# x's half of each state-space group and B and C projected as columns: the weights as stationary operand, 256 tokens moving

## The chip, the cores and the metric

One core of a Trainium2 chip runs the whole layer. The metric is the device time of one execution in microseconds (us). Five engines work beside each other and meet at semaphores: TensorE (PE in the profile, its weight loads PEld), VectorE (DVE), ScalarE (ACT), GpSimd (POOL) and SyncE (SP, which issues DMAs).

## What is computed

A decoder layer over 256 tokens of width 2048, in float32: a combined input projection, a Mamba-2 state-space branch beside a differential attention branch, gates, an output projection and a SwiGLU. The change concerns the input projection of the state-space branch and the convolution behind it:

```python
h = rms_norm(x, mix_norm_w[layer], NORM_EPS)
proj = jnp.einsum('bsd,dn->bsn', h, w_in[layer])
z, xbc, dt_raw, q, k, v, g_ssm, g_att = jnp.split(proj, splits, axis=-1)
...
xbc = jax.nn.silu(causal_depthwise_conv(xbc, conv_w, conv_b))
xs, Bm, Cm = jnp.split(xbc, [SSM_D_INNER, SSM_D_INNER + G * N], axis=-1)
```

The convolution has four taps along the tokens and is separate for each of the 6144 channels of xbc: 4096 of x (8 groups of 512), 1024 of B and 1024 of C.

## The kernel before, in words

**Products in three parts.** Every float32 matrix is split into a high part, rounded to float32r, and a low part, the rest. A product is three matmuls: high by high, high by low, low by high. The normed tokens h are kept transposed, as `h_hi` and `h_lo` (128 channels on the partitions, 16 k-tiles, 256 tokens); the norm's factor of each token (`x_rstd`, a column over tokens) is applied to the product afterwards, since h is stored without it.

**Units.** The weights stream in units of two k-tiles by 512 columns (`UK` = 2, `CW` = 512, 512 KB). SyncE loads a unit to `w_raw`, ScalarE rounds it to `w_hi` (`split_hi`, line 722), VectorE subtracts to get `w_lo` (`split_lo`, line 1246), TensorE multiplies (`rows_unit`, line 2233). Each of these has a ring of four slots (`RING` = 4): a split waits until the unit four before it is through TensorE, a load until its slot is split. A chunk is 8 units (`UPC`): 512 output columns for all 256 tokens, in one of two accumulators `acc[0]`, `acc[1]` in PSUM (two banks each, one for each 128 tokens). `acc_free` guards them. ScalarE and VectorE run through the units four ahead of TensorE (`LEAD` = 4); in their programs the end of a chunk (`chunk_done`) stands behind the split of the fourth unit of the next one.

In `rows_unit` the tokens are stationary: for each k-tile and each 128 tokens, three matmuls with 128x128 stationary tokens and 512 moving weight columns, 12 matmuls a unit. The result has tokens on the partitions ("rows").

**The order of the program.** q and k (8 chunks), v (in a form with seven products), then 8 chunks with the 16 attention heads' work between their units: first four chunks of B and C, then four of gates. Then four chunks of a projection of the attention's result, then the groups: for each of 8 groups a chunk of x in `acc[0]` and a chunk of z in `acc[1]`, the repeated ones in a loop of 7. Then the second gates, the projections and the SwiGLU. Between the units of a chunk small pieces of other work are put in by hand (`heads_between`, `branch_between`, `z_between`, `tail_between`).

**From rows to channels.** The convolution needs the channels on the partitions. So for B and C ScalarE copies `acc` to `bc_row`, scaled by `x_rstd`; some chunks later TensorE transposes it in pieces of 128x128 into the PSUM tile `side` (`bc_columns`, after the third unit of each of the four chunks of the attention's projection), ScalarE computes the first tap out of `side` (`conv_first_taps`, line 836) and VectorE the other three (`conv_other_taps`, line 1436). For x ScalarE copies `acc[0]` to `x_proj` (line 956), TensorE transposes `x_proj` back into `acc[0]` after the first unit of the z chunk (`z_between`, u == 0, eight transposes), and the taps read `acc[0]`, which is released after the last tap. A transpose is line 2249 in the profile.

**What follows in a group** (`z_between`, `z_chunk`, `x_chunk`). Still at u == 0 TensorE computes C by B (`cb`, lines 2572 and 2573) and transposes `y_row`, the normed result of the group before, which waits for VectorE's `tail_normed` (line 1611), that for GpSimd's rsqrt, and that for ScalarE's squares. VectorE's taps come behind its split of the fifth z unit. Behind them come ScalarE's silu and exponentials (`exps`, line 968), VectorE's `decays` (line 1645) and `xdt` (line 1669), ScalarE's copy to `y_row` and GpSimd's step on it (line 2186), each between splits. In the next x chunk, behind the third and fourth unit, TensorE runs the y products (`y_products`, line 2534) and VectorE `tail_gated`. GpSimd masks the decays of the next group (line 2180) meanwhile.

**dt** has 64 channels and is projected before the change as columns already (line 2463): 64 stationary weight columns, 256 moving tokens.

## Time and profile before

| | us |
|---|---|
| median of 3 runs (lowest, highest) | 2055.84 (2054.61, 2057.56) |
| the profiled execution, its own time | 2056.46 |
| its span in the trace | 2054.8 |
| TensorE busy | 2046.9 |
| TensorE's weight loads busy | 1688.1 |
| VectorE busy | 1565.0 |
| ScalarE busy | 1164.2 |
| GpSimd busy | 170.3 |

The span is divided among stages: q and k, v, attention with B, C and the first gates to about 500 us, the attention's projection to about 594 us, the groups from 594 to 1029 us, and from there the second gates, projections and the SwiGLU. Busy times of TensorE are from modelled ends: what one matmul costs is read from the distance of two starts. A group of instructions gives a line of the kernel, an engine, an operation and tiles, as `out<-in`, its count and the mean of one. A timeline row gives start, length and what was waited for; neighbouring rows of one kind are merged (x8).

### The profile page before, as it was taken

The numbers are of one execution on the slowest core, as the hardware profiler recorded it, in microseconds if no ns is written. First come the engines' busy times: TensorE is split into PE (matmuls) and PEld (weight loads), VectorE is DVE, ScalarE is ACT, GpSimd is POOL, SyncE is SP. The second block draws the span as 40 slices with busy tenths as digits, with TensorE's granted clock in tenths as the row PEclk, the third lists the DMA queues.
The fourth block names the chain that finished last, engine by engine and source line by source line (L and its number), as shares of the span: only waits on it lengthen the run. The fifth ranks groups of instructions, "written<-read, shape, count | busy, mean of one in ns | idle before, by whom it ended". The sixth has DMA issues, their size and how long they took to land.

```text
span 2054.8 us, 27952 instructions
## 1 busy us (share of the span) xinstructions
PE 2046.9 (100%) x9530; PEld 1688.1 (82%) x9530; DVE 1565.0 (76%) x1860; ACT 1164.2 (57%) x1488; POOL 170.3 (8%) x195
## 2 busy tenths in 40 slices
PE   9999999999999999999999999999999999999999
PEld 8888877778888888888888888888888888887887
DVE  6777866665866777777767887898898889877866
ACT  5444655555556666666655454566666666645543
POOL 1121000000011222222100000000000000000000
PEclk9999999999999999999999999999999999999999
DMA  7656675554566665555565657598888888666574
GB/s 250 198 180 205 194 215 165 173 168 144 183 204 184 184 184 184 184 184 184 165 193 184 211 169 246 174 306 246 258 253 239 251 257 250 198 202 229 180 240 153
DMA packets 220627, 419.80 MB, mean 204 GB/s; under 512 B 16450, under 2 KB 22003, under 8 KB 220291
## 3 DMA queue, kind: packets, MB, share of 16 engines
q1 hardware_dynamic: 212162, 399.48, 61.1%
q0 software_dynamic: 7776, 18.94, 4.3%
q8 instruction: 47, 0.77, 0.2%
q10 hardware_dynamic: 608, 0.34, 0.1%
q14 instruction: 34, 0.27, 0.0%
HBM read 410.25 MB, written 4.26 MB: 202 GB/s over the span
## 4 chain that ended last, share of the span: by engine, by line
PE 97%; DVE 2%; DMA 1%; ACT 0%; issue 0%; SPq 0%; DVEq 0%; ACTq 0%
PE acc L2233 75%; PE side L2320 9%; PE acc L2320 6%; PE side L2249 3%; PE side L2534 1%; DVE w_lo L2025 1%; PE side L2389 1%; DMA w_raw<-in_w_ffn_down 1%; DVE w_raw L1940 0%; DMA x_row<-in_x 0%; PE side L2540 0%; PE acc L2249 0%; PE side L2463 0%; ACT w_hi L1205 0%; PE side L2404 0%
## 5 line engine op out<-in xcount | busy, mean ns | idle before, releaser
L1246 DVE TENSOR_TENSOR w_lo<-w_raw,w_hi 128x1024 fp32r<-128x1024 f32 x332 | 418.9, 1277 | 250.1 <-ACT w_hi L722 248.9
L722 ACT ACTIVATE w_hi<-w_raw 128x1024 fp32r<-128x1024 f32 x332 | 347.9, 1057 | 373.1 <-PE acc L2233 319.4
L2233 PE MATMUL acc<-w_hi,h_hi 128*128 128x512 f32 x1248 | 498.4, 399 | 0.2
L2233 PE MATMUL acc<-w_hi,h_lo 128*128 128x512 f32 x1248 | 487.2, 390 | 0.0
L2233 PE MATMUL acc<-w_lo,h_hi 128*128 128x512 f32 x1248 | 486.0, 389 | 0.0
L2233 PEld LDWEIGHTS acc<-w_hi,h_hi 128*128 128x128 f32 x1248 | 234.4, 188 | 51.0 <-issue 5.6
L2233 PEld LDWEIGHTS acc<-w_hi,h_lo 128*128 128x128 f32 x1248 | 234.2, 188 | 50.4
L2233 PEld LDWEIGHTS acc<-w_lo,h_hi 128*128 128x128 f32 x1248 | 234.7, 188 | 47.9 <-issue 1.9
L1919 DVE TENSOR_TENSOR w_lo<-w_raw,w_hi 128x1024 fp32r<-128x1024 f32 x136 | 165.3, 1222 | 38.0 <-ACT w_hi L1126 35.4
L1042 ACT ACTIVATE w_hi<-w_raw 128x1024 fp32r<-128x1024 f32 x110 | 116.4, 1060 | 116.1 <-PE acc L2233 71.5
L1126 ACT ACTIVATE w_hi<-w_raw 128x1024 fp32r<-128x1024 f32 x136 | 142.9, 1057 | 66.4 <-PE acc L2233 50.9
L1205 ACT ACTIVATE w_hi<-w_raw 128x1024 fp32r<-128x1024 f32 x102 | 107.6, 1060 | 106.6 <-DMA w_raw<-in_w_ffn_down 56.4
L1721 DVE TENSOR_TENSOR w_lo<-w_raw,w_hi 128x1024 fp32r<-128x1024 f32 x110 | 132.5, 1223 | 45.6 <-ACT w_hi L1042 43.6
L1126 ACT ACTIVATE w_hi<-side_raw 128x1024 fp32r<-128x1024 f32 x100 | 106.2, 1062 | 96.6 <-PE acc L2233 45.8
L2025 DVE TENSOR_TENSOR w_lo<-w_raw,w_hi 128x1024 fp32r<-128x1024 f32 x102 | 122.6, 1223 | 48.7 <-ACT w_hi L1205 47.5
L2233 PE MATMUL acc<-w_hi,x2T_hi 128*128 128x512 f32 x384 | 150.7, 392 | 0.0
L2233 PE MATMUL acc<-w_hi,x2T_lo 128*128 128x512 f32 x384 | 149.6, 390 | 0.0
L2233 PE MATMUL acc<-w_lo,x2T_hi 128*128 128x512 f32 x384 | 149.4, 389 | 0.0
L1919 DVE TENSOR_TENSOR w_lo<-side_raw,w_hi 128x1024 fp32r<-128x1024 f32 x100 | 122.2, 1222 | 17.9 <-ACT w_hi L1126 16.3
L2233 PE MATMUL acc<-w_hi,a_hi 128*128 128x512 f32 x252 | 98.2, 390 | 0.0
L2233 PE MATMUL acc<-w_hi,a_lo 128*128 128x512 f32 x252 | 98.1, 389 | 0.0
L2233 PE MATMUL acc<-w_lo,a_hi 128*128 128x512 f32 x252 | 98.0, 389 | 0.0
(434 smaller groups left out, 3458.6 us busy)
## 6 DMA issues: line engine op xcount, KB each, us to landing
w_raw<-in_w_in SPq DMA_DIRECT2D x320, 512.0 KB, 4.3
w_raw<-in_w_ffn_down SPq DMA_DIRECT2D x88, 512.0 KB, 4.9
w_raw<-in_w_ffn_gate SPq DMA_DIRECT2D x68, 512.0 KB, 4.5
w_raw<-in_w_ffn_up SPq DMA_DIRECT2D x68, 512.0 KB, 5.3
w_raw<-in_w_ssm_proj SPq DMA_DIRECT2D x64, 512.0 KB, 4.4
side_raw<-in_w_ffn_up SPq DMA_DIRECT2D x40, 512.0 KB, 4.6
w_raw<-in_w_attn_proj SPq DMA_DIRECT2D x32, 512.0 KB, 3.7
w_raw<-in_w_out SPq DMA_DIRECT2D x32, 512.0 KB, 4.8
```

The source lines that it names most:

```text
L722: nc.scalar.activation(w_hi[:, r], w_raw[:, n % RING], ACT.Copy).then_inc(hi_ready, 1)
L1042: nc.scalar.activation(w_hi[:, unit.slot % RING], w_raw[:, source], ACT.Copy).then_inc(hi_ready, 1)
L1126: nc.scalar.activation(w_hi[:, unit.slot % RING], ffn_source(names, name), ACT.Copy).then_inc(hi_ready, 1)
L1205: nc.scalar.activation(w_hi[:, unit.slot % RING], w_raw[:, source], ACT.Copy).then_inc(hi_ready, 1)
L1246: nc.vector.tensor_tensor(w_lo[:, r], w_raw[:, n % RING], w_hi[:, r].bitcast(F32), ALU.subtract).then_inc(lo_ready, 1)
L1721: nc.vector.tensor_tensor(w_lo[:, r], w_raw[:, source], w_hi[:, r].bitcast(F32), ALU.subtract).then_inc(lo_ready, 1)
L1919: nc.vector.tensor_tensor(w_lo[:, r], ffn_source(names, names[n]), w_hi[:, r].bitcast(F32), ALU.subtract).then_inc(lo_ready, 1)
L2025: nc.vector.tensor_tensor(w_lo[:, r], w_raw[:, source], w_hi[:, r].bitcast(F32), ALU.subtract).then_inc(lo_ready, 1)
L2233: done = nc.tensor.matmul(acc[p][:, t], a[:, k0 + kk, cut], w[:, r, kk], start=first and kk == n == 0, stop=last and kk == UK - 1 and n == ...
L2249: return nc.tensor.transpose(out_at, in_, ident)
L2320: done = nc.tensor.matmul(out_at, a, w[:, r, kk], start=first and kk == n == 0, stop=last and kk == UK - 1 and n == 2, skip_group_check=se ...
L2389: last = nc.tensor.matmul(side[:, 1 + m, first:first + width], qkT[half, 0, q * P:(q + 1) * P], qkT[half, 1, 0:width], start=True, stop=True)
```

## The change

B, C and x are projected as columns from the start. `columns_unit` takes 128 weight columns as the stationary operand and all 256 tokens as the moving one: for each of 2 k-tiles, 4 column tiles and 3 products one matmul of 128x256, 24 a unit. The result has channels on the partitions, two column tiles in each bank of `acc`. VectorE multiplies it by the token factors, which now have to stand as a row on all partitions (`rstd_row`, `x_rstd_row`), and writes `bc_cols` or `x_cols` in SBUF; the taps read these. The transposes, ScalarE's scaled copies and the waits for them go. `acc[0]` is released after VectorE's product, not after the last tap. The row of factors is made once: VectorE puts `x_rstd` on diagonals, TensorE multiplies them by ones (`rstd_rows`, after the seventh unit of the second chunk), ScalarE copies the result out of `side`.

```diff
+                    if second and u == UPC - 1:
+                        act.wait_ge(rows_T, 2)
+                        act.wait_ge(norms_in, 3 * 16)
+                        nc.scalar.activation(rstd_row[:], side[:, 1, 0:T], ACT.Copy).then_inc(cols_ready, 1)
...
                 for c in range(2):
                     chunk_with_heads(i * 4 + 2 * c)
-                    for t in range(TT):
-                        last = nc.scalar.activation(bc_row[:, t, bass.ds(i * (2 * CW) + c * CW, CW)], acc[c][:, t], ACT.Copy,
-                                                    scale=x_rstd[:, t:t + 1])
-                    last.then_inc(acc_free[c], 1)
...
+            nc.scalar.activation(x_rstd_row[:], rstd_row[:], ACT.Copy).then_inc(acs_ready, 1)
...
-                chunk_done()
-                for t in range(TT):
-                    last = nc.scalar.activation(x_proj[:, t], acc[0][:, t], ACT.Copy, scale=x_rstd[:, t:t + 1])
-                last.then_inc(x_rows_ready, 1)
...
-                        act.wait_ge(x_T, g + 1)
+                        act.wait_ge(x_cols_ready, g + 1)
                         for n in range(CT):
-                            last = conv_first_taps(sums(0)[:, n], g * CT, conv_x[:, n], n)
+                            last = conv_first_taps(x_cols[:, n], g * CT, conv_x[:, n], n)
...
+                    if second and u == LEAD + 1:
+
+                        dve.wait_ge(rstd_ready, TT)
+                        for t in range(TT):
+                            last = nc.vector.tensor_scalar(rstd_diag[:, t], ident, x_rstd[:, t:t + 1], None, ALU.mult)
+                        last.then_inc(lam_sums, 1)
...
                 for c in range(2):
                     chunk_with_heads(i * 4 + 2 * c)
+                    chunk_done()
+                    nc.vector.tensor_tensor(bc_cols[:, bass.ds(i * (2 * CT) + c * CT, CT)], sums(c),
+                                            rstd_row[:].unsqueeze(1).broadcast_to([P, CT, T]), ALU.mult).then_inc(bc_cols_ready, 1)
+                    dve.wait_ge(bc_cols_ready, i * 2 + (c + 1))
+                    nc.vector.sem_inc(acc_free[c], 1)
...
+                dve.wait_ge(mm_done, unit.now(-LEAD))
+                nc.vector.tensor_tensor(x_cols[:], sums(0), x_rstd_row[:].unsqueeze(1).broadcast_to([P, CT, T]), ALU.mult).then_inc(x_cols_ready, 1)
+                dve.wait_ge(x_cols_ready, g + 1)
+                nc.vector.sem_inc(acc_free[0], 1)
...
-                    if u == 2:
-
-                        dve.wait_ge(conv_done, g + 1)
-                        nc.vector.sem_inc(acc_free[0], 1)
...
+            def columns_unit(p, k0, first, last):
+
+                r = unit.slot % RING
+                pe.wait_ge(lo_ready, unit.step())
+                for kk in range(UK):
+                    for n in range(CT):
+                        cut = slice(n * P, (n + 1) * P)
+                        for m, (w, a) in enumerate(((w_hi, h_hi), (w_hi, h_lo), (w_lo, h_hi))):
+                            done = nc.tensor.matmul(acc[p][:, n // 2, n % 2 * T:(n % 2 + 1) * T], w[:, r, kk, cut], a[:, k0 + kk],
+                                                    start=first and kk == m == n % 2 == 0, stop=last and kk == UK - 1 and m == 2,
+                                                    skip_group_check=True)
+                done.then_inc(mm_done, 1)
...
+            def rstd_rows():
+                pe.wait_ge(lam_sums, 3)
+                for t in range(TT):
+                    last = nc.tensor.matmul(side[:, 1, t * P:(t + 1) * P], ones[:], rstd_diag[:, t], start=True, stop=True)
+                last.then_inc(rows_T, 1)
...
-                        chunk(c, h_hi, h_lo, between=heads_between(i * 4 + (8 * n + 2 * c)))
+                        if n == 0:
+                            chunk_of_columns(c, between=heads_between(i * 4 + (8 * n + 2 * c)))
+                        else:
+                            chunk(c, h_hi, h_lo, between=heads_between(i * 4 + (8 * n + 2 * c)))
...
-                    if u == 2:
-                        bc_columns(c)
...
-                        pe.wait_ge(x_rows_ready, g + 1)
-                        for n in range(CT):
-                            for t in range(TT):
-                                at_col = (n % 2) * T + t * P
-                                last = transpose(acc[0][:, n // 2, at_col:at_col + P], x_proj[:, t, n * P:(n + 1) * P])
-                        last.then_inc(x_T, 1)
                         pe.wait_ge(bT_ready, g + 1)
...
-            chunk(0, h_hi, h_lo)
+            chunk_of_columns(0)
             chunk(1, h_hi, h_lo, between=z_between(0, True))
             with repeat(pe, G - 1, [(unit, 2 * UPC), (pair, 1)]) as i:
-                chunk(0, h_hi, h_lo, between=tail_between(i))
+                chunk_of_columns(0, between=tail_between(i))
                 chunk(1, h_hi, h_lo, between=z_between(i + 1))
```

In the order of instructions TensorE has in the repeated group, around the end of the first z unit, before the change (line 2233 is the row form's matmul, stationary operand last; 2249 a transpose; ISA and REGISTER_ALU compute addresses and counts):

```order
L2233 MATMUL acc<-w_hi,h_lo 128x512
L2558 REGISTER_ALU
L2249 MATMUL acc<-ident,x_proj 128x128 x8
L2572 ISA
L2572 MATMUL side<-bc,bT 128x256
L2573 ISA
L2573 MATMUL side<-bc,bT 128x128
L2249 MATMUL side<-ident,y_row 128x128 x8
```

and the same place of the changed program:

```order
L2249 MATMUL acc<-w_hi,h_lo 128x512
L2597 REGISTER_ALU
L2605 ISA
L2605 MATMUL side<-bc,bT 128x256
L2606 ISA
L2606 MATMUL side<-bc,bT 128x128
L2288 MATMUL side<-ident,y_row 128x128 x8
```

x's eight transposes are gone, and y_row's stand directly behind the two small products. VectorE, from the norming of y_row to the first tap, before:

```order
L1611 TENSOR_SCALAR y_row<-y_row,small 128x512 x2
L1245 REGISTER_ALU
L1246 TENSOR_TENSOR w_lo<-w_raw,w_hi 128x1024
L1245 REGISTER_ALU
L1246 TENSOR_TENSOR w_lo<-w_raw,w_hi 128x1024
L1652 REGISTER_ALU
L1436 ISA
L1436 SCALAR_TENSOR_TENSOR conv_x<-acc,taps,conv_x 128x255
```

and in the changed program:

```order
L1624 TENSOR_SCALAR y_row<-y_row,small 128x512 x2
L1245 REGISTER_ALU
L1246 TENSOR_TENSOR w_lo<-w_raw,w_hi 128x1024
L1646 TENSOR_TENSOR x_cols<-acc,x_rstd_row 128x1024
L1647 REGISTER_ALU
L1245 REGISTER_ALU
L1246 TENSOR_TENSOR w_lo<-w_raw,w_hi 128x1024
L1442 ISA
L1442 SCALAR_TENSOR_TENSOR conv_x<-x_cols,taps,conv_x 128x255
```

One product of 128x1024 has come in between the splits of the fourth and the fifth z unit, and the taps read x_cols in place of the accumulator.

## Rows read from the trace of the kernel before

**Rows 1.** The page: busy times, the chain's engines, and SyncE's loads of w_in
```profile
PE 2046.9 (100%) x9530; PEld 1688.1 (82%) x9530; DVE 1565.0 (76%) x1860; ACT 1164.2 (57%) x1488; POOL 170.3 (8%) x195
...
PE 97%; DVE 2%; DMA 1%; ACT 0%; issue 0%; SPq 0%; DVEq 0%; ACTq 0%
...
w_raw<-in_w_in SPq DMA_DIRECT2D x320, 512.0 KB, 4.3
```
**Rows 2.** Windows: length, then PE, PEld, DVE, ACT, POOL busy, granted clock, DMA
```profile
616.00:1016.00 400.00, 399.88 (x1979) 335.39 (x1978) 288.55 (x312) 250.78 (x393) 85.82 (x65) 1.00 0.60 183
```
**Rows 3.** Who waited for whom, 600 to 1020 us, TensorE's entry for y_row
```profile
PEld side L2249 <- DVE y_row L1611: 0.3, 1, 0.3
```
**Rows 4.** TensorE's timeline in the row form's stream, tenth start after the first
```profile
843.98 0.39 PE L2233 MATMUL acc<-w_hi,h_hi 128*128 128x512 f32 x1
...
846.02 0.39 PE L2233 MATMUL acc<-w_hi,h_hi 128*128 128x512 f32 x1
```
**Rows 5.** TensorE's timeline in dt's products (64 stationary columns, 256 moving)
```profile
494.92 0.28 PE L2463 MATMUL side<-h_hi,wdt_lo 128*64 128x256 f32 x1
...
495.94 0.28 PE L2463 MATMUL side<-h_hi,wdt_lo 128*64 128x256 f32 x1
```
**Rows 6.** Weight loads of three lines (ns), decay's matmuls, and a sequencer's instruction
```profile
L2463 PEld LDWEIGHTS side<-h_hi,wdt_lo x16: 133/134/135, 494.8 to 499.9; 128*64 128x64 f32 x16
...
L2233 PEld LDWEIGHTS acc<-w_lo,h_hi 128*128 128x128 f32 x520 | 97.7, 188 | 21.3 <-issue 1.9
...
L2534 PE MATMUL side<-xdt,decay 128*128 128x64 f32 x256 | 30.3, 271 | 0.0
...
647.61 1.89 PE L2534 MATMUL side<-xdt,decay 128*128 128x64 f32 x16
...
L2573 PEldq FUSED_REGOPS  x7: 51/51/51, 668.5 to 977.2; - x7
```
**Rows 7.** TensorE's timeline behind the first z unit, in two of the repeated groups
```profile
670.28 1.09 PE L2249 MATMUL side<-ident,y_row 128*128 128x128 f32 x8
...
771.56 1.04 PE L2249 MATMUL acc<-ident,x_proj 128*128 128x128 f32 x8
772.44 0.60 PE L2572 MATMUL side<-bc,bT 128*128 x2
...
773.09 1.04 PE L2249 MATMUL side<-ident,y_row 128*128 128x128 f32 x8
```
**Rows 8.** VectorE's timeline in the same two groups
```profile
667.21 3.01 DVE L1611 TENSOR_SCALAR y_row<-y_row,small 128x512 f32<-128x512 f32 x2
...
769.18 3.02 DVE L1611 TENSOR_SCALAR y_row<-y_row,small 128x512 f32<-128x512 f32 x2
772.13 2.35 DVE L1246 TENSOR_TENSOR w_lo<-w_raw,w_hi 128x1024 fp32r<-128x1024 f32 x2
774.95 5.24 DVE L1436 SCALAR_TENSOR_TENSOR conv_x<-acc,taps,conv_x 128x255 f32<-128x255 f32 x12 [0.47 <-ACT conv_x L836]
...
781.24 1.22 DVE L1617 TENSOR_TENSOR yT<-side,cols 128x1024 f32 x1
...
796.43 1.32 DVE L1246 TENSOR_TENSOR w_lo<-w_raw,w_hi 128x1024 fp32r<-128x1024 f32 x1 [1.22 <-ACT w_hi L722]
```
**Rows 9.** GpSimd's timeline in the second of them
```profile
764.73 6.79 POOL L2180 TENSOR_TENSOR acs_b<-acs_b,cst 128x1024 f32<-128x1024 f32 x2
```
**Rows 10.** ScalarE's first taps and silu, and TensorE behind the next x chunk's third unit
```profile
772.86 1.93 ACT L836 ACTIVATE conv_x<-acc,cols,taps 128x256 f32<-128x256 f32 x4
...
780.61 1.04 ACT L986 ACTIVATE conv_x<-conv_x 128x1024 f32<-128x1024 f32 x1
...
802.13 1.89 PE L2534 MATMUL side<-xdt,decay 128*128 128x64 f32 x16
```
**Rows 11.** ScalarE and VectorE around the seventh unit of the second chunk
```profile
54.37 1.06 ACT L722 ACTIVATE w_hi<-w_raw 128x1024 fp32r<-128x1024 f32 x1 [1.42 <-PE acc L2233]
...
52.74 1.23 DVE L1246 TENSOR_TENSOR w_lo<-w_raw,w_hi 128x1024 fp32r<-128x1024 f32 x1 [0.63 <-ACT w_hi L722]
```

More of the change, by code:

```diff
@@ L271, in layer @@
         acs_b = at("acs_b", 179, [P, 2, HG // 2, T])
-        x_proj = at("x_proj", 187, [P, TT, CW])
+        x_cols = at("x_cols", 187, [P, CT, T])
+        x_rstd_row = at("x_rstd_row", 175, [P, T])
         conv_x = at("conv_x", 191, [P, CT, T])
@@ L906, in _ @@
                     if u == 2:
[L907 removed]
+                        act.wait_ge(bc_cols_ready, c + 1)
                         for n in range(CT):
[L909 removed]
+                            last = conv_first_taps(bc_cols[:, c * CT + n:c * CT + n + 1], c * CT + DI // P, bc[:, c * CT + n:c * CT + n + 1], n)
                         last.then_inc(bc_first, 1)
@@ L1578, in _ @@
                         for n in range(CT):
-                            last = conv_other_taps(side_columns()[:, n], c * CT + DI // P, bc[:, c * CT + n], n, back)
+                            last = conv_other_taps(bc_cols[:, c * CT + n], c * CT + DI // P, bc[:, c * CT + n], n, back)
                         if back < TAPS - 1:
@@ L1628, in x_chunk @@
                             tail_normed(g - 1)
+                if head:
+                    dve.wait_ge(acs_ready, 3)
+                dve.wait_ge(mm_done, unit.now(-LEAD))
+                nc.vector.tensor_tensor(x_cols[:], sums(0), x_rstd_row[:].unsqueeze(1).broadcast_to([P, CT, T]), ALU.mult).then_inc(x_cols_ready, 1)
+                dve.wait_ge(x_cols_ready, g + 1)
+                nc.vector.sem_inc(acc_free[0], 1)
             def conv_taps(g, back):
                 for n in range(CT):
-                    last = conv_other_taps(sums(0)[:, n], g * CT, conv_x[:, n], n, back)
+                    last = conv_other_taps(x_cols[:, n], g * CT, conv_x[:, n], n, back)
                 if back < TAPS - 1:
@@ L2246, in chunk, with chunk_of_columns @@
                     pair.step()
+            def columns_unit(p, k0, first, last):
[9 more added lines that the diff above has]
+                done.then_inc(mm_done, 1)
+            def chunk_of_columns(p, between=None):
+                pe.wait_ge(acc_free[p], pair.now(1))
+                for u in range(UPC):
+                    columns_unit(p, u * UK, u == 0, u == UPC - 1)
+                    if between is not None:
+                        between(u)
+                if p:
+                    pair.step()
             def transpose(out_at, in_):
```

18 lines of the change are left out of this document (7 added, 11 removed).

## The prediction, made before the changed kernel ran

> **What bounds the kernel now.** I read the page first, then the windows, then who waited for whom, then matmul starts one by one. TensorE is busy 2046.9 of 2054.8 us and the chain that ended last is 97% TensorE [rows 1]; in the state-space stretch, 616 to 1016 us, it is busy 399.9 of 400 us at a granted clock of 1.00 (its 2.4 GHz level), while VectorE is busy 72% and ScalarE 63% of it [rows 2]. Hardly anything waits on TensorE: the longest entry for a matmul outside the kernel's ends is a 0.3 us wait for y_row [rows 3]. So what TensorE has to issue is the time, and the other engines count only where they come too late for it. The spacing of matmuls is therefore what I price. In the main stream (512 moving columns, a weight load of 128 columns each) ten starts span 843.98 to 846.02, nine steps: 0.2267 us each [rows 4]. A unit of two k-tiles has 12 of them, 2.72 us.
>
> **The stream itself.** Twelve chunks change form: four of B and C, and x's chunk in each of eight groups. Each has 8 units, so 12 x 8 x 12 = 1152 matmuls of 512 columns become 2304 of 256, with twice as many weight loads. Per matmul there is now one load of 128 columns for 256 moving ones. No row has just this form. Three come near it:
> - dt's products stream 256 columns past weights of 64 columns, nine steps from 494.92 to 495.94: 0.1133 us each [rows 5], exactly half of 0.2267.
> - A load of 64 columns is 134 ns long, one of 128 columns 188 ns [rows 6]: 54 ns for 64 columns, so 128 columns take about 108 ns and a fixed part of some 80 ns that can overlap.
> - Where loads of 128 columns are what limits (decay's matmuls with 64 moving columns), 16 matmuls take 1.89 us, the last one 0.27 of it: 1.62/15 = 0.108 us each [rows 6].
>
> So load (0.108) and stream (0.1133) each fit into 0.1133 us, with some 5 ns to spare. I take 0.1133, since the row with 256 moving columns is nearest in what streams, and the change of the stream is 2304 x 0.1133 - 1152 x 0.2267 = 0. The bound above: 512 columns at 2.4 GHz are 213.3 ns, so 13.4 ns are extra beside a load of 128 columns; 256 columns are 106.7, and 6.7 ns are extra beside a load of 64. The extra may thus go with the moving columns (my choice) or with the loaded ones; in the second case the new matmul takes 106.7 + 13.4 = 0.120 us. A gain has its bound at 106.7 ns, which would give 15 us; the row of 256 columns with only half the load doesn't reach that, so I leave it out.
>
> The Trainium skill (TensorE: Matmul & The Clock Gate, Back-to-back issue gap) gives a gap of N/2.4 ns plus a fixed 2.5 ns per matmul. By that rule 1152 more matmuls would add an estimated 2.9 us to the sum. The trace doesn't show a fixed part for this type: 0.1133 is half of 0.2267.
>
> **Removed from TensorE.** Eight transposes per chunk: x_proj's burst starts at 771.56, what follows it at 772.44, 0.88 us [rows 7]. B and C have four such bursts between units: 3.5 us, all of it on the path. x has eight: 7.0 us, if TensorE finds the next thing ready.
>
> It does so only in part. Behind x's transposes come two small products and then the transposes of y_row, which wait for VectorE's normed y_row. In the group at 770 these start at 773.09, and VectorE ended at 769.18 + 3.02 = 772.20 [rows 7, 8], 0.89 before: nearly all of the 0.88 may be used. That VectorE step is long because GpSimd is masking until 771.52 [rows 9], and its time hangs on TensorE's earlier y products, so it doesn't move forward. In the first repeated group it ends at 670.22 and the transposes start at 670.28 [rows 7, 8]: there all 0.88 are lost. Of the seven repeated groups four are like the one at 772 (0.1 lost each, for the release), one is the one at 670, and two lie between (I take 0.3 each): 0.88 + 0.6 + 0.4 = 1.9 us lost.
>
> **Moved.** ScalarE's two scaled copies of the accumulator become one VectorE product of 128x1024 out of PSUM, for which the nearest row is yT's, 1.22 us [rows 8]. It stands behind the split of the fourth z unit, so it would run from 773.3 to 774.5; ScalarE's four first taps wait for it and take 1.93 us [rows 10]; so VectorE's other taps start at about 776.5 instead of 774.95 [rows 8], 1.6 us later. Queued behind them are the z splits, the decays, xdt, and then the splits of the next x chunk. ScalarE already keeps silu waiting about 0.4 us (780.19 to 780.61 [rows 8, 10]) for another split, so some 1.2 us of delay go down the chain. Where does that reach TensorE? The tightest place I find is the split of the third unit of the next x chunk: it runs from 796.43 to 797.75 [rows 8] and TensorE takes it 2.72 us before 802.13 [rows 10], at 799.4. That is 1.7 us of cover; 1.2 later on one side and 0.8 earlier on the other leave TensorE waiting about 0.3 us, in eight groups 2.4 us. Bounds: nothing, if taps read from SBUF are shorter than from PSUM, and 0.64 us a group, where x's whole gain (5.1 us by then) is gone. The rest of x's gain: 7.0 - 1.9 - 2.4 = 2.7 us.
>
> SyncE's loads follow VectorE's splits, so they are issued up to 1.6 us later in that part of the group; half a megabyte of w_in lands 4.3 us after issue [rows 1] and the units concerned are due ten later, so I cost this at nothing. GpSimd's step on y_row also moves 1.2 us, into time in which it idles. In B and C's chunks VectorE's new product comes after the chunk's last split, with four units (10.9 us) split ahead: nothing.
>
> **Added once.** The row of x's scales: two VectorE products, two TensorE ones (each issued as two instructions, about 0.11 us each, 0.45 with the change of form) after the seventh unit of the second chunk. TensorE gets there at about 54.2, when ScalarE's split behind that unit starts (54.37) [rows 11]; VectorE's products come behind its split of 52.74 + 1.23 = 53.97 and end about 54.5: 0.3 us of wait. Together 0.8 us.
>
> **Sum.** 2056.46 (the profiled execution; its span is 2054.8) + 0 - 3.5 - 2.7 + 0.8 = 2051.1. The median of the runs, 2055.84, is 0.6 lower, so I predict **2050.5 us**. The forecast's own range, with 0 to 0.6 us of wait a group, is 2048 to 2053.
>
> **The rivals.**
> - The extra of the matmul goes with the load (0.120 us): 2304 x 0.0067 = +15.4 us. TensorE is then slower in just these chunks, most of the waits above vanish, and the gain is 3.5 + 7.0 - 1.9 - 0.8 = 7.8. Median 2055.84 + 15.4 - 7.8 = **2063.4**, slower. It decides from 0.1168 us per matmul on (7.8/2304 = 3.4 ns more than 0.1133). For it: the same rows [4, 5] fit it as well. Against: with 128 columns loaded per 0.108 us nothing of the sort shows at decay's matmuls. Chance 0.17.
> - A small cost per unit that 512 columns hid. In a loop TensorE's sequencer also computes what to wait for; such an instruction lasts 51 ns [rows 6], and between two 512-column matmuls there were over 100 ns of room for it, now 5. At 96 units, 51 ns each: +4.9, so **2055.4**, no change. Chance 0.17.
> - VectorE's chain takes x's whole gain, 0.64 us a group or more, and leaves B's and C's 3.5 less 0.8: **2053**, no change. Chance 0.10.
> - Loads aren't hidden at all. The price, as a mechanism here: 0.108 us of load before each of the 2304 matmuls, +249 us, so **2305**. Against it: at 0.2267 us a matmul, 213 of streaming and 108 of load can't stand one behind the other [rows 4, 6]. Chance 0.02.
>
> By the Trainium skill (same page, The mechanism, What overlaps and what doesn't) a weight load overlaps matmuls in flight only when its row group differs, which all these loads, over 128 rows, don't. By that rule the time would be that last one; the trace disagrees, with 0.2267 us for both.
>
> **How the numbers follow.** The forecast has 0.54, the rivals 0.17, 0.17, 0.10 and 0.02. A measurement can tell about 0.2%, 4.1 us: faster is below 2051.7, slower above 2060. Of the forecast's 0.54 about 0.46 lie below 2051.7. Same: the rest of it, most of the second rival and the third, 0.31. Slower: 0.23, the first and last rival and a little of the second. The range reaches from the forecast without its waits for splits (2.4) and most of those for y_row (1.9) to just above the first rival: 2046.5 to 2064.5.
>
> **What would show it.** In the changed profile, matmuls with 256 columns should stand 0.1133 us apart: 0.120 shows the first rival, 0.1133 with a step at every unit the second. VectorE's taps on conv_x should begin some 7.7 us after the first z matmul starts (now 774.95 less 768.84, which is a unit before 771.56: 6.1). The waits on TensorE should now list y_row, and splits (w_lo) at the third unit of an x chunk, a few tenths each. Group periods should shrink from 51.4 us (670.28 to 773.09 is two [rows 7]) by 0.3 to 0.8. I am wrong if the spacing is off by over 3 ns, or if TensorE waits for w_lo for over 1 us a group.

## The result, and the profile after the change

| | us |
|---|---|
| changed kernel, median of 5 runs (lowest, highest) | 2067.7 (2065.22, 2069.38) |
| kernel before, median of 5 runs beside them | 2055.84 (2054.61, 2057.56) |
| ratio, 95% interval | 1.0052 (1.0040 to 1.0064) |
| the profiled execution, its own time and its span | 2069.38, 2067.8 |

The change makes the kernel 0.5% slower, by 11.9 us between the medians, by 10.7 (8.2 to 13.2) as the ratio and its interval have it, and by 12.9 between the two profiled executions. 2050.5 was predicted, and the time lies above the range (2046.5 to 2064.5), beyond the first rival's 2063.4.

The page after the change, answering to [rows 1]: busy times, the chain's engines and SyncE's loads.

```profile
PE 2054.7 (99%) x10590; PEld 1740.8 (84%) x10590; DVE 1581.5 (76%) x1874; ACT 1151.9 (56%) x1466; POOL 170.6 (8%) x195
...
PE 83%; DVE 8%; issue 3%; DMA 3%; ACT 2%; DVEq 0%; ACTq 0%; SPq 0%; POOLq 0%
...
w_raw<-in_w_in SPq DMA_DIRECT2D x320, 512.0 KB, 4.0
```

The chain was 97% TensorE and is now 83%, with 8% VectorE and 3% DMA in it. So two things changed: TensorE has more to issue (busy 7.8 us longer), and it now waits for others. The stretch of the groups, answering to [rows 2], says the second:

```profile
616.00:1016.00 400.00, 394.15 (x2531) 355.17 (x2531) 293.86 (x314) 235.82 (x370) 83.13 (x65) 1.00 0.58 177
```

394.15 of 400 us busy, where it was 399.88, at the same granted clock of 1.00. ScalarE lost its copies (250.78 to 235.82) and VectorE got its product (288.55 to 293.86), as the change says.

TensorE's timeline after the change, from the second matmul of an x chunk's fifth unit to the first of the sixth, 23 steps:

```profile
656.07 0.28 PE L2272 MATMUL acc<-h_lo,w_hi 128*128 128x256 f32 x1
656.19 0.28 PE L2272 MATMUL acc<-h_hi,w_lo 128*128 128x256 f32 x1
...
658.82 0.28 PE L2272 MATMUL acc<-h_hi,w_hi 128*128 128x256 f32 x1
```

2.75 us for 23 steps is 0.1196 us a matmul, where 0.1133 was my choice and 0.120 the first rival's price. The waits of TensorE are the entries that answer to [rows 3] (engine and tile that waited, for whom: us in all, times, the longest). The last line is the same wait for y_row as its weight loads have it, from 600 to 1040 us, in all seven repeated groups:

```profile
PE side L2288 <- DVE y_row L1624: 3.0, 6, 0.6
PE side L2288 <- DVE yT L1630: 2.8, 7, 0.4
...
PEld side L2288 <- DVE y_row L1624: 4.4, 7, 0.8
```

And TensorE's timeline in one repeated group, at the places of [rows 7]: the first matmul of the z chunk, the small products behind the first z unit, y_row's transposes, and later conv_x's.

```profile
826.06 0.40 PE L2249 MATMUL acc<-w_hi,h_hi 128*128 128x512 f32 x1
...
828.81 0.59 PE L2605 MATMUL side<-bc,bT 128*128 x2
829.24 0.38 PE L2606 MATMUL side<-bc,bT 128*128 x2
830.11 1.09 PE L2288 MATMUL side<-ident,y_row 128*128 128x128 f32 x8 [0.49 <-DVE y_row L1624]
...
841.73 0.39 PE L2249 MATMUL acc<-w_hi,h_lo 128*128 128x512 f32 x1
842.52 1.06 PE L2288 MATMUL side<-ident,conv_x 128*128 128x128 f32 x8 [0.40 <-DVE yT L1630]
```

x's eight transposes are gone. y_row's start 0.87 us after the second small product, where 0.22 is usual (in the run tail_early 775.23 to 775.45, below): 0.65 of wait. conv_x's start 0.79 after the last matmul ahead of them, where a matmul of 512 takes 0.23: 0.56 of wait. Before the change they started without one, 0.23 behind the matmul ahead of them (784.66 to 784.89).

These transposes ask for two things: for conv_x itself, which is ScalarE's silu, and for VectorE's product yT, which has to be through with reading the columns of `side` that they write. ScalarE and VectorE in the same group:

```profile
840.14 1.06 ACT L986 ACTIVATE conv_x<-conv_x 128x1024 f32<-128x1024 f32 x1 [2.36 <-DVE conv_x L1442]
```
```profile
841.16 1.21 DVE L1630 TENSOR_TENSOR yT<-side,cols 128x1024 f32 x1
```

Silu is done at 841.18, and yT at 842.37, 0.15 before the transposes start. So the wait is for yT, as the profile says, and not for silu. yT stands on VectorE behind the taps and one split, and it has come later with them.

A group, from one state update's y products to the next, was 51.4 us long and is 53.1 in the middle of the loop:

```profile
760.56 1.08 PE L2579 MATMUL side<-xdt_end,cb 128*128 128x512 f32 x2
...
813.64 1.08 PE L2579 MATMUL side<-xdt_end,cb 128*128 128x512 f32 x2
```

The account of such a group: the stream 192 x (0.120 - 0.1133) = +1.28, the transposes -0.88, the two waits +0.65 and +0.56, together +1.6 of the +1.7. In the first two of the seven repeated groups the wait for y_row is shorter, 0.2 and 0.4.

B's and C's chunks are another matter. TensorE's products of q and k for the heads stand at the same place in each chunk of that stretch; from the first of them to the last of the fifth chunk, so over 30 of the 32 units of B and C, before and after:

```profile
L2389 PE MATMUL side<-qkT x80: 272/374/378, 277.8 to 394.1; 64*128 64x128 f32 x40, 64*128 64x256 f32 x40
```
```profile
L2436 PE MATMUL side<-qkT x80: 272/374/378, 279.2 to 397.8; 64*128 64x128 f32 x40, 64*128 64x256 f32 x40
```

116.3 us have become 118.6: +2.3, where 30 x 24 x 0.0067 = +4.8 would be the price. The traces of bc_only, reord, tail_early and tail_reord (below) have 118.5 to 118.7, those of x_only, before_y and rows_stream, with the row form here, 116.2 to 116.3. Between the heads' work the row form is itself slower than 0.2267, 0.229 in the ten steps from 321.44 to 323.73 of the kernel before; that is a part of the difference, and the rest is not taken apart. So the stream costs 8 x 1.28 = 10.2 in x and some 2.5 in B and C, 12.7 us in all.

### The profile page after: what moved, and what is told of

Its sections match the earlier page's. It is cut to its first block, busy times and chain, and to the rows that moved or that the text cites. A ratio compares the mean times of both kernels' runs of the same rounds, so it can differ in the third digit from the quotient of the medians.

```text
span 2067.8 us, 30069 instructions
## 1 busy us (share of the span) xinstructions
PE 2054.7 (99%) x10590; PEld 1740.8 (84%) x10590; DVE 1581.5 (76%) x1874; ACT 1151.9 (56%) x1466; POOL 170.6 (8%) x195
## 4 chain that ended last, share of the span: by engine, by line
PE 83%; DVE 8%; issue 3%; DMA 3%; ACT 2%; DVEq 0%; ACTq 0%; SPq 0%; POOLq 0%
PE acc L2249 52%; PE acc L2272 12%; PE side L2367 7%; PE acc L2367 5%; PE side L2288 2%; PE side L2573 1%; DVE w_lo L1246 1%; DVE w_lo L2041 1%; DMA w_raw<-in_w_ffn_down 1%; DVE w_lo L1737 1%; DVE conv_x L1442 1%; DMA w_raw<-in_w_ssm_proj 1%; PE side L2436 1%; DVE w_lo L1935 1%; ACT w_hi L725 1%
## 5 line engine op out<-in xcount | busy, mean ns | idle before, releaser
L2249 PE MATMUL acc<-w_hi,h_hi 128*128 128x512 f32 x864 | 342.4, 396 | 0.2
L2249 PE MATMUL acc<-w_hi,h_lo 128*128 128x512 f32 x864 | 337.0, 390 | 0.0
L2249 PE MATMUL acc<-w_lo,h_hi 128*128 128x512 f32 x864 | 336.5, 389 | 0.0
L2272 PE MATMUL acc<-h_hi,w_hi 128*128 128x256 f32 x768 | 223.8, 291 | 0.0
L2272 PE MATMUL acc<-h_hi,w_lo 128*128 128x256 f32 x768 | 217.2, 283 | 0.0
L2272 PE MATMUL acc<-h_lo,w_hi 128*128 128x256 f32 x768 | 217.1, 283 | 0.0
L2249 PEld LDWEIGHTS acc<-w_hi,h_hi 128*128 128x128 f32 x864 | 162.3, 188 | 34.4 <-issue 1.9
L2249 PEld LDWEIGHTS acc<-w_hi,h_lo 128*128 128x128 f32 x864 | 162.2, 188 | 34.6
L2249 PEld LDWEIGHTS acc<-w_lo,h_hi 128*128 128x128 f32 x864 | 162.4, 188 | 32.0 <-issue 0.2
L1042 ACT ACTIVATE w_hi<-w_raw 128x1024 fp32r<-128x1024 f32 x110 | 116.3, 1060 | 117.4 <-PE acc L2249 60.2
L2272 PEld LDWEIGHTS acc<-h_hi,w_hi 128*128 128x128 f32 x768 | 147.0, 191 | 3.8 <-issue 3.3
```

Source lines behind the costliest of these rows:

```text
L1042: nc.scalar.activation(w_hi[:, unit.slot % RING], w_raw[:, source], ACT.Copy).then_inc(hi_ready, 1)
L2249: done = nc.tensor.matmul(acc[p][:, t], a[:, k0 + kk, cut], w[:, r, kk], start=first and kk == n == 0, stop=last and kk == UK - 1 and n == ...
L2272: done = nc.tensor.matmul(acc[p][:, n // 2, n % 2 * T:(n % 2 + 1) * T], w[:, r, kk, cut], a[:, k0 + kk], start=first and kk == m == n % 2 ...
```

## The experiments

The theory after the result: (a) a float32r matmul with 256 moving columns and 128 stationary ones costs 0.120 us, which takes back more than the transposes gave; (b) the rest are two waits in a group, made by the new order of VectorE's work. Each run is told as a ratio to the kernel before, in runs on the same chip (medians of before 2057.0 to 2057.9 there).

**m1_bursts and m2_bursts: the disputed cost by itself.** The kernel before, with bursts of 36 independent matmuls at its end, on data that is ready:

```diff
+            for columns, tokens in ((128, 512), (128, 384), (128, 256), (96, 256), ...):
+                for n in range(36):
+                    nc.tensor.matmul(side[0:columns, n % 4, 0:tokens], w_hi[:, n % RING, 0, 0:columns],
+                                     a_hi[:, n % 8:n % 8 + 2].rearrange("p k t -> p (k t)")[:, 0:tokens], start=True, stop=True)
```

> The kernel before, with bursts of 36 matmuls added behind its last output, S stationary columns by N moving columns, float32r, results unused. Theory L (each loaded column takes 0.104 ns from the stream, so a matmul is N/2.4 + 0.104 S ns): 128 by 512 226.7 ns from start to start, 128 by 384 173.3, 128 by 256 120.0, 96 by 256 116.7, 64 by 256 113.3, 32 by 256 110.0, 96 by 512 223.3, 64 by 512 220.0, 32 by 512 216.7, 128 by 128 the pace of loads alone, 108 to 112, 64 by 128 60. Theory P (the extra goes with the moving columns, 0.443 ns each, and 128 by 256 is held at 120 by how fast 128 columns can be loaded beside a stream): 226.7, 170.0, 120, then 113.3 for 96, 64 and 32 by 256, 226.7 for 96, 64 and 32 by 512, 120 for 128 by 128, 57 to 60 for 64 by 128. The two part at 32 by 512: 216.7 against 226.7.

The groups of the first run's bursts, different shapes apart (busy us of 36, mean ns of one):

```profile
L2778 PE MATMUL side<-a_hi,w_hi 128*128 128x384 f32 x36 | 6.4, 335 | 0.0
L2778 PE MATMUL side<-a_hi,w_hi 128*128 128x256 f32 x36 | 4.5, 282 | 0.0
L2778 PE MATMUL side<-a_hi,w_hi 128*96 128x256 f32 x36 | 4.3, 278 | 0.0
L2778 PE MATMUL side<-a_hi,w_hi 128*64 128x256 f32 x36 | 4.2, 276 | 0.0
L2778 PE MATMUL side<-a_hi,w_hi 128*32 128x256 f32 x36 | 4.2, 276 | 0.0
L2778 PE MATMUL side<-a_hi,w_hi 128*128 128x128 f32 x36 | 4.1, 273 | 0.0
L2778 PE MATMUL side<-a_hi,w_hi 128*64 128x128 f32 x36 | 2.3, 222 | 0.0
```

The theories part at 32 by 512: 216.7 or 226.7 ns. It came out at 231.7, so neither holds. A burst of 256 columns takes 0.3 us longer past 128 stationary columns than past 64, some 7 ns a matmul. Between 64 and 32 there is no difference. With 128 moving columns the load is the limit (4.1 us against 2.3 with half of it).

> The kernel before with other bursts behind its end. If a matmul takes the largest of 0.443 N, N/2.4 + 0.104 S, and 0.87 S (loads alone) ns: 128 by 448 200.1, 128 by 320 146.7, 128 by 224 111.7, 112 by 256 118.4, 80 by 256 115.0, 96 by 384 170.0, 64 by 384 170.0, 128 by 192 111.7. If the load costs only when it leaves under some time free (theory P), 128 by 448 is 198.3 and 80 by 256 113.3.

Both runs together (one execution each, at a granted clock of 1.00), ns from start to start, from the single records of each burst; in brackets what lies above the moving columns at 2.4 GHz:

| stationary columns | 512 moving | 448 | 384 | 320 | 256 | 224 | 192 | 128 |
|---|---|---|---|---|---|---|---|---|
| 128 | 227.0 (13.7) | 202.7 (16.0) | 173.4 (13.4) | 146.7 (13.4) | 120.0 (13.3) | 111.6 (18.3) | 111.8 | 111.7 |
| 112 | | | | | 113.3 (6.6) | | | |
| 96 | 230.0 (16.7) | | 175.0 (15.0) | | 115.9 (9.2) | | | |
| 80 | | | | | 113.3 (6.6) | | | |
| 64 | 230.3 (17.0) | | 173.3 (13.3) | | 113.3 (6.6) | | | 60.0 |
| 32 | 231.7 (18.4) | | | | 113.3 (6.6) | | | |

With 128 stationary columns 13.3 ns or a little more lie on every matmul, whatever its length from 256 to 512: a fixed part. It is neither proportional to the moving columns, as my choice had it, nor does it follow from the loaded ones alone, as the rival had it: at 384 and 512 it stays with a narrow load. It shrinks, to 6.6 ns (9.2 at 96), only with 256 moving columns past fewer than 128 stationary ones, and one of these is dt's form, the one row that I took my price from. Two matmuls of 256 therefore pay twice what one of 512 pays. Why the fixed part is there isn't known.

**bc_only and x_only: one half of the change each.** The hunks for B and C alone, and those for x alone, with the row of factors in both.

> Only B and C projected as columns (4 chunks), x as before. Theory L or P: 4 x 192 matmuls x 6.6 ns = +5.1, transposes -3.5, the row of factors +0.8, no new wait: 2055.8 + 2.4 = 2058.2 us. Rival: most of the loss is from VectorE's new products in the attention stretch holding up its heads: then clearly more than +5.

> Only x projected as columns (8 chunks), B and C as before. Theory: 8 x 192 x 6.6 ns = +10.1, transposes -7.0, new waits of TensorE for y_row 0.45 and for the transposes of conv_x 0.56 in 7 groups = +7.1, row of factors +0.8: +11.0, 2066.8 us. Rival (the waits only stand where time would be lost anyway): +4, 2060.

bc_only: 1.0009 (1.0000 to 1.0018), +1.9 us (0 to 3.7). x_only: 1.0049 (1.0035 to 1.0063), +10 (7.2 to 13). Both times are near what was expected, but bc_only doesn't show the terms. Its sum was +5.1 - 3.5 + 0.8 = +2.4; with B's and C's stream at 2.5 it is -0.2, just below the interval. Its profiled execution, 2.7 us above the median, has something more: the first repeated group is 55.1 us long, where it was 51.7, with a wait of 1.9 us for y_row behind a late load of w_in. How often that comes, one trace can't tell. x carries most of the loss, and alone it shows TensorE's wait ahead of conv_x's transposes in all seven repeated groups, but the one for y_row once:

```profile
PE side L2287 <- DVE yT L1629: 2.7, 7, 0.4
...
PE side L2287 <- DVE y_row L1623: 0.6, 1, 0.6
```

The groups of x_only are 52.3 to 52.9 us long. Why y_row's wait is mostly absent, the run tail_early below helps to see: `tail_gated` begins 2.0 to 2.3 us after the y products in six of the seven groups, and 2.9 in the one with the wait of 0.6; in the changed kernel it is 2.3 to 2.9. Why the load that it stands behind comes earlier in x_only is open.

**reord: the two waits taken away by order.** VectorE's product for x comes ahead of its split of the fourth z unit, and y_row's transposes come behind the second z unit:

```diff
-                        if not first:
-                            y_columns(g - 1)
+                    if u == 1 and not first:
+                        y_columns(g - 1)
...
                 for u in range(UPC):
+                    if u == UPC - 1:
...
+                        nc.vector.tensor_tensor(x_cols[:], sums(0), ...).then_inc(x_cols_ready, 1)
                     split_lo()
```

> The changed kernel with two pieces moved: VectorE's product of x ahead of its split of the fourth z unit (1.1 us earlier), and TensorE's transposes of y_row behind the second z unit in place of the first. If the two waits (0.45 and 0.56 us a group) are what the other engines add, both vanish: 2067.7 - 7.1 = 2060.6 us. Rival (the chain of VectorE and ScalarE is the bound of a group, and a wait comes back at the next splits): 2064 or more. Matmul spacing stays 0.120 in both.

1.0019 (1.0010 to 1.0028): 6.8 us of the 10.7 that the ratio of the changed kernel stands for. The two waits sum up to 8 us in the trace of the changed kernel, and 0.9 us of them (for yT, in two groups) are still there. So (b) holds within the intervals. What is left is near the stream less the transposes.

**before_y: the same move of y_row's transposes in the kernel before.**

> The kernel before with the transposes of y_row behind the second z unit in place of the first. It takes away the one wait of 0.3 us and, where the spacing is not the matter, nothing else: 2055.5 us, no change. If y_row's wait had been hidden in more groups than the trace shows, up to 2 us less.

1.0000 (0.9991 to 1.0009). The move alone brings nothing where there is no wait.

**tail_early: which step makes y_row late.** In the kernel before, VectorE's `tail_gated` runs as soon as TensorE's y products are there. ScalarE, VectorE and TensorE in one group of the kernel before:

```profile
807.34 1.06 ACT L722 ACTIVATE w_hi<-w_raw 128x1024 fp32r<-128x1024 f32 x1 [3.95 <-DMA w_raw<-in_w_in]
```
```profile
808.43 1.23 DVE L1246 TENSOR_TENSOR w_lo<-w_raw,w_hi 128x1024 fp32r<-128x1024 f32 x1 [3.40 <-ACT w_hi L722]
809.65 0.69 DVE L1597 TENSOR_TENSOR xdt_end<-side,edge 128x512 f32<-128x512 f32 x1
```
```profile
808.41 1.08 PE L2540 MATMUL side<-xdt_end,cb 128*128 128x512 f32 x2
```

and in the changed kernel, where the y products start at 813.64 (the row is above):

```profile
814.16 1.06 ACT L725 ACTIVATE w_hi<-w_raw 128x1024 fp32r<-128x1024 f32 x1 [4.21 <-DMA w_raw<-in_w_in]
```
```profile
815.26 1.23 DVE L1246 TENSOR_TENSOR w_lo<-w_raw,w_hi 128x1024 fp32r<-128x1024 f32 x1 [3.67 <-ACT w_hi L725]
816.40 0.68 DVE L1610 TENSOR_TENSOR xdt_end<-side,edge 128x512 f32<-128x512 f32 x1
```

Measured from the start of the y products, `tail_gated` begins after 1.24 us before the change (809.65 less 808.41, 0.16 behind their end) and after 2.76 in the changed kernel, since it is queued behind the split of x's eighth unit, ScalarE's half of which waits for the load of w_in. Against the y products, that load has slipped by 1.6 us (from 1.07 us ahead of them to 0.52 behind). That is this group; over the seven, `tail_gated` begins 1.24 to 2.68 us after the y products before the change and 2.31 to 2.92 after it. The edit takes `tail_gated` out of that queue:

```diff
                 for u in range(UPC):
+                    if not head and u == 3:
+                        tail_gated(g - 1)
                     split_lo()
                     if not head:
-                        if u == 3:
-                            tail_gated(g - 1)
```

> The changed kernel with one move: in x's chunk VectorE's first step on the gated y (tail_gated, which reads y_sum's result and xdt_end) comes ahead of the split of x's eighth unit, not behind it. Theory (y_row's transposes wait on TensorE since tail_gated stands behind a split that waits for the load of w_in): tail_gated begins right at TensorE's y products again, some 1.5 us earlier, and the wait of 0.65 us at y_row's transposes in seven groups goes: -4.5 us against the changed kernel, about 2063, ratio 1.003. The wait for conv_x stays (0.56 a group) or grows by up to 0.3, since the split of the eighth unit comes later and with it the chain behind: then -2.5, ratio 1.004. Rival (y_row is late through GpSimd's mask or through the split work as a whole): nothing moves, ratio 1.005.

1.0031 (1.0019 to 1.0043), the theory's number. The interval touches that of the changed kernel, so it is the trace that decides: groups of 52.1 us in place of 53.1, the wait for y_row gone in all seven, and the one ahead of conv_x's transposes shrunk, from 0.56 to 0.33, where it was expected to stay or grow. The same place as above:

```profile
775.23 0.38 PE L2606 MATMUL side<-bc,bT 128*128 x2
775.45 1.04 PE L2288 MATMUL side<-ident,y_row 128*128 128x128 f32 x8
...
787.01 0.39 PE L2249 MATMUL acc<-w_hi,h_lo 128*128 128x512 f32 x1
787.57 1.06 PE L2288 MATMUL side<-ident,conv_x 128*128 128x128 f32 x8 [0.18 <-DVE yT L1630]
```

**tail_reord: both orders together, the best form of the change that computes everything.**

> The moves of tail_early and of reord together on the changed kernel, all values computed. Theory: reord had left hardly a wait on TensorE (0.9 us for yT in two groups), so this is the same as reord, 2061 to 2062, ratio 1.002, and the form's cost of 0.4 us per column chunk is what remains. Rival (loads and splits are late through tail_gated, and reord kept part of it as small waits): 1 to 2 us under reord, ratio 1.001. Neither gives a ratio under 1.

1.0017 (1.0008 to 1.0026). Its stretch of the groups has no idle left, and its groups are 51.73 us long:

```profile
616.00:1016.00 400.00, 400.00 (x2584) 362.80 (x2583) 293.54 (x318) 243.02 (x377) 88.85 (x65) 1.00 0.58 181
```

51.4 + 1.28 - 0.88 = 51.8: with all waits gone, the group is what TensorE has to issue, and that is more than before the change. No order helps against this. The whole kernel closes too: 12.7 for the stream, -10.5 for the transposes and +0.8 for the row of factors are +3.0, and the ratio stands for +3.5 (1.6 to 5.3). With 15.4 for the stream it would be +5.7, above that interval.

**rows_stream, rows_reord, rows_tail: the change with the cost of the form taken out.** The matmuls of the column chunks have the old form again, 12 of 512 moving columns a unit. Everything around them is as changed, so B, C and x get values that aren't theirs.

```diff
-                    for n in range(CT):
-                        cut = slice(n * P, (n + 1) * P)
-                        for m, (w, a) in enumerate(((w_hi, h_hi), (w_hi, h_lo), (w_lo, h_hi))):
-                            done = nc.tensor.matmul(acc[p][:, n // 2, n % 2 * T:(n % 2 + 1) * T], w[:, r, kk, cut], a[:, k0 + kk], ...)
+                    for t in range(TT):
+                        cut = slice(t * P, (t + 1) * P)
+                        for m, (a, w) in enumerate(((h_hi, w_hi), (h_hi, w_lo), (h_lo, w_hi))):
+                            done = nc.tensor.matmul(acc[p][:, t], a[:, k0 + kk, cut], w[:, r, kk], ...)
```

> The changed kernel with only its stream put back: the 12 chunks use 12 matmuls of 512 moving columns a unit again, and all else (VectorE's products, taps from SBUF, no transposes) is as changed. It leaves out the turning to channels, so the values behind it are those of rows taken for columns. If the spacing of 0.120 in place of 0.1133 is the loss, 2304 x 6.6 ns = 15.2 us go: 2067.7 - 15.2 = 2052.5 us, faster than before by 3. Rival (VectorE's chain holds the groups, whatever the stream): TensorE waits more as it gets faster, and 2056 or more remains.

1.0033 (1.0021 to 1.0045), a clear miss of the theory: with 12.7 us less to issue (15.2 by the expectation), the kernel is only some 4 us faster than the changed one, and still slower than before. Its waits on TensorE:

```profile
PE side L2287 <- DVE y_row L1624: 6.6, 7, 1.6
...
PE side L2287 <- DVE yT L1630: 2.7, 7, 0.4
```

The wait for y_row was 3.0 us in the changed kernel and is 6.6 here, so the slow stream had covered a part of it; the one for yT is what it was. So my sum would have failed with its own price of the matmul too. rows_reord adds the two moves of reord, rows_tail that of tail_early as well:

> The changed kernel with both edits at once: the column chunks' matmuls have the old form again (512 moving columns, 8 of 12 streams of work as before; the values of B, C and x are then not the reference's, since rows are taken for columns), and the two moves of the run reord are in: VectorE's product for x ahead of the split of the fourth z unit, TensorE's transposes of y_row behind the second z unit. Theory (the form costs 6.6 ns for each of 2304 matmuls, the waits in the groups are the rest): the change's transposes are saved in full, -10.5 +0.8, and no wait is left, so 2055.84 - 9.7 = 2046.1, ratio 0.9953; and against the run reord -15.2 or, from its 2061.69 less 0.4 of a later session, about 2046. Rival (the groups are held by VectorE's and ScalarE's chain, which the slower stream had only hidden): the group period stays over 51 us, as in rows_stream, and the run ends at 2055 or above, ratio 0.999 or more. Between the two: each group keeps some 0.3 us of wait, 2048.5.

> The run rows_reord (the column chunks' matmuls in the old form, so B, C and x are not the reference's; VectorE's product for x and TensorE's transposes of y_row moved) plus the move of tail_early (tail_gated ahead of the split of x's eighth unit). rows_reord ended at 2056.5 where 2046.1 was expected; its groups are 51.0 to 51.8 us long, where 50.5 would be what TensorE has to issue. Theory (the whole chain of ScalarE's and VectorE's splits and taps from the x product to the split of the third unit of the next x chunk is what holds the fast form; in rows_reord TensorE waits 0.3 us there for w_lo in a group, and this move does nothing to it): no gain against rows_reord, 2055 to 2057.5, ratio 0.999 to 1.0005. Rival (the waits come from y's tail behind the load of w_in, as in the changed kernel itself): the groups shrink to some 50.6 us, 2050, ratio 0.9965.

rows_reord: 0.9996 (0.9987 to 1.0005), the rival's number. rows_tail: 0.9978 (0.9969 to 0.9987), faster than before by 4.5 us and between its two theories. Its groups are all 51.2 us long, where 50.5 would be the issue alone. That closes as well: -10.5 + 0.8 and seven groups of some 0.7 us of wait are -4.8, so the transposes' 10.5 us are there to be had. TensorE's timeline of rows_reord at the start of the third unit of the next x chunk:

```profile
796.75 0.39 PE L2272 MATMUL acc<-w_hi,h_lo 128*128 128x512 f32 x1
797.25 0.50 PE L2272 MATMUL acc<-w_hi,h_hi 128*128 128x512 f32 x1
797.59 0.40 PE L2272 MATMUL acc<-w_lo,h_hi 128*128 128x512 f32 x1
```

0.50 us from 796.75 to 797.25 where 0.23 is the step: a wait of 0.27 for the split of just that unit, which rows_tail has at the same place. Of the other 0.4 a group in rows_tail, 0.1 is the longer step right behind this wait (797.25 to 797.59 here), and nearly 0.2 is the wait ahead of conv_x's transposes again, 0.42 where 0.23 is the step, in each of the seven groups:

```profile
780.30 0.39 PE L2249 MATMUL acc<-w_hi,h_lo 128*128 128x512 f32 x1
780.72 1.07 PE L2287 MATMUL side<-ident,conv_x 128*128 128x128 f32 x8
```

Some 0.1 a group stays open.

**wide_pairs: could the form be mended?** On top of reord, `h_hi` and `h_lo` stand side by side, so that one load of w_hi serves 512 moving columns, and w_lo has 256: 16 matmuls a unit in place of 24. The low product lands in the neighbouring half, so the values aren't the reference's.

```diff
+                        nc.tensor.matmul(acc[p][:, n // 2].rearrange("p (h t) -> p h t", h=2), w_hi[:, r, kk, cut], h_both[:, :, k0 + kk], ...)
+                        done = nc.tensor.matmul(acc[p][:, n // 2, n % 2 * T:(n % 2 + 1) * T], w_lo[:, r, kk, cut], h_hi[:, k0 + kk], ...)
```

> reord with a third of the loads gone: the high part of the weights is loaded once and the high and low part of h stream past it as one matmul of 512 columns, into the whole bank, then the low part of the weights by 256 columns. It leaves out the adding of the two halves (the product with h's low part falls into the neighbouring tile's sum), so its values are not the reference's. If a matmul takes the larger of 0.443 N and N/2.4 + 0.104 S ns, three of 120 become 226.7 + 120 = 346.7 ns: 12 chunks x 64 x 13.3 ns = -10.2 us against reord, that is 2049.5 us beside 2055.8 of before. Rival (a cost per matmul of 256, whatever is loaded): -7.7 less what the wide one costs, near the same; rival (loads have no part in it, the columns form as such is slow): no change against reord.

1.0005 (0.9995 to 1.0014), some 3 us under reord where 10.2 were expected. A pair is 0.347 us (656.31 to 659.43 is nine pairs):

```profile
656.31 0.40 PE L2271 MATMUL acc<-h_both,w_hi 128*128 128x512 f32 x1
656.54 0.28 PE L2273 MATMUL acc<-h_both,w_lo 128*128 128x256 f32 x1
...
659.43 0.39 PE L2271 MATMUL acc<-h_both,w_hi 128*128 128x512 f32 x1
```

A pair is 13 ns shorter than three matmuls at 0.120, so one fixed part is saved in each, 768 x 0.0133 = 10.2 us in all. The stream gave what was expected; most of it didn't reach the end. Waits came back, the largest in the groups the one for yT ahead of conv_x's transposes (2.2 us in five of them). No version tried that computes everything beats the kernel before.

## Why the prediction was wrong, step by step

The forecast was 17.2 us too low. The stream, put at 0, cost some 12.7. And x, of whose 7.0 us for the transposes 4.3 were to be lost in waits, lost 4.4 for y_row and 7 x 0.56 = 3.9 for yT, 8.3 in all: 4.0 more. Together that is 16.7.

- **"I take 0.1133": the term that was mis-sized.** The stream was put at 0. At the measured spacing it would cost 2304 x (0.1196 - 0.1133) = +14.5 us, or +15.4 with the bursts' 0.120; of that 10.2 came in x's chunks and some 2.5 in B's and C's. I had two rows that fitted two readings, and chose "the row with 256 moving columns" since it "is nearest in what streams". In stationary columns it was the farthest, and it was the one form with half the fixed part. The first rival had the spacing exactly (0.120), though not its reason. The bound deserved more weight: 15.4 us is nearly six times the 2.7 that I forecast for x. The pace of loads alone, read as 0.108 at decay's matmuls, was low too: it is 111.7 ns in the bursts.
- **The fixed part per matmul.** I wrote "The trace doesn't show a fixed part for this type: 0.1133 is half of 0.2267". The bursts show one, 13.3 ns. The Trainium skill (TensorE: Matmul & The Clock Gate, Back-to-back issue gap) has a rule of this kind, N/2.4 plus a constant of 2.5 ns, for the gap of a single matmul. The runs here show 13.3, and the measurement decides: my estimate by it was +2.9 us, in the right direction and under a quarter of what came.
- **Removed transposes: right.** x's 0.88 a group is confirmed by tail_reord's period, and all 10.5 us together by the sums of tail_reord and rows_tail. B's and C's 3.5 alone no run sets apart.
- **The row of factors, 0.8: right,** both parts. VectorE's products follow its split at 54.07, and TensorE's four start 0.53 behind the last matmul, a 0.3 us wait, and take 0.47:

```profile
54.07 0.39 PE L2249 MATMUL acc<-w_hi,h_lo 128*128 128x512 f32 x1
54.60 0.71 PE L2346 MATMUL side<-rstd_diag,ones 128*128 128x128 f32 x4
55.07 0.48 PE L2249 MATMUL acc<-w_hi,h_hi 128*128 128x512 f32 x1
```

- **y_row, "1.9 us lost": wrong in size and reason.** It was 4.4. I took its time to hang on TensorE's y products and so to stand still. It hung on a load as well: "SyncE's loads follow VectorE's splits ... so I cost this at nothing" is the step that failed. The load slipped by 1.6 us against the y products, as much as I had worked out for VectorE's taps ("1.6 us later"), and `tail_gated` is queued behind the split that needs it. I had asked when the late load's own unit is due on TensorE, ten units on, and not what stands behind its split on VectorE.
- **"leaves TensorE waiting about 0.3 us" for the third x unit: the mechanism was right, its place in the changed kernel not.** The changed kernel has no such wait; its slower stream covers it. With the fast stream it appears exactly there, 0.27 us. "The tightest place I find" is the step that failed. There was a tighter one on the same chain: yT, behind the taps and a split, which conv_x's transposes wait for, 0.56 us a group. Before the change yT ended at 781.24 + 1.22 = 782.46 [rows 8] and the transposes came at 784.89, 2.4 us of cover; the 1.6 us that I had worked out for the taps and the 0.88 of the removed transposes use all of that. And the taps came later still: they begin 8.8 us after the first z matmul (826.06 to 834.82, below), not 7.7, since VectorE's product for x stands behind the norming of y_row, and that is late too.
- **Rivals.** The first was said to make "most of the waits above vanish". They did not: its own sum without waits is 15.4 - 10.5 + 0.8 = +5.7, the stream that came makes it +3.0, and some 8 us of waits bring that to the measured 10.7 to 11.9. The second (a cost per unit) isn't there: 656.07 to 658.82 runs across a unit's border at the even step of 0.12. The third (VectorE's chain takes x's gain) was right as a mechanism and too small at its price: in rows_stream -9.7 us without waits became +6.8. The fourth rival is excluded: 0.120 us holds a load and its matmul.

## What to carry to other kernels

Halving the moving columns doubles whatever each matmul costs besides its columns, so price a new form of matmul by a row with the same stationary width as well as the same moving width, or by a burst, before anything else; a difference of 7 ns a matmul, 12.7 us in all, outweighed the 10.5 of all transposes that the new form saved. When a change makes one engine's chain later, ask for every delayed load what stands behind its consumer in that engine's queue, and for every delayed step all that waits for it, also where it only has to be through with reading a buffer. And a slower stream hides waits: undo the slow part alone, and the waits that it hid come out.

## What was not expected of the hardware

- A float32r matmul with 128 stationary columns takes its moving columns at 2.4 GHz plus some 13.3 ns for 256 to 512 of them (120.0, 146.7, 173.4 and 227.0 ns); only 448 had more, 16.0.
- The load alone sets 111.7 ns a matmul with 128 stationary columns and 60.0 with 64, when 128 columns move.
- Narrower stationary data makes a matmul of 256 columns shorter (113.3 in place of 120.0), one of 512 longer (230 in place of 227).
- Taps that read SBUF are no shorter than those that read PSUM: VectorE's twelve take 5.29 us in place of 5.24 and ScalarE's four 2.08 in place of 1.93 [rows 8, 10].

```profile
834.82 5.29 DVE L1442 SCALAR_TENSOR_TENSOR conv_x<-x_cols,taps,conv_x 128x255 f32<-128x255 f32 x12 [1.03 <-ACT conv_x L843]
```
```profile
832.57 2.08 ACT L843 ACTIVATE conv_x<-x_cols,cols,taps 128x256 f32<-128x256 f32 x4 [2.50 <-DVE x_cols L1646]
```
